# Opening modulation blocks in two halves, and another order of the steps in neighbourhood attention

## The reference

```python
shift, scale, gate = jnp.split(jax.nn.silu(cond) @ w_mod + b_mod, 3, axis=-1)   # cond: c or c_ctx
h = rms_norm(x, g_pre) * (1 + scale) + shift
(sg_u, sg_v, sg_gate, dq, dk, dv, d_gate, nq, nk, nv, n_gate, f_gate, merge) = split(h @ w_in)
y_sg   = spatial_gating(sg_u, sg_v, ...)            # A
y_diff = diff_attention(dq, dk, dv, lam)            # B
y_na   = neighbourhood_attention(nq, nk, nv, ...)   # C: 8 heads, 256 local keys per query tile + 128 cached
y_f    = fourier_mix(h)                             # D
mixed = sum over the branches of sigmoid(merge_i) * ((y_i * silu(gate_i)) @ p_i)
out = rms_norm(mixed @ w_o, g_post);   return x + gate * out
```

## Time and profile before

| | us |
|---|---|
| median of 3 runs | 2064.86 (2063.15 to 2065.28) |
| the profiled execution | 2058.49 |
| its span | 2056.4 |
| TensorE busy in it | 1963.3 |
| VectorE, ScalarE, GpSimd busy | 955.7, 647.1, 593.6 |

### The profile page before, as it was taken

How to read it: one execution, slowest core, us unless ns; L and a number is a source line. 1 busy time by engine, 2 the same in 40 slices (tenths; PEclk the granted TensorE clock), 3 DMA queues, 4 the chain that set the end, 5 groups by cost and what they waited for, 6 DMA issues and landing times.

```text
span 2056.4 us, 30590 instructions
## 1 busy us (share of the span) xinstructions
PE 1963.3 (95%) x12384; PEld 1782.0 (87%) x12384; DVE 955.7 (46%) x1480; ACT 647.1 (31%) x1101; POOL 593.6 (29%) x278
## 2 busy tenths in 40 slices
PE   6799989999999999999999999999999999999998
PEld 3698877889898999999878988888988899999996
DVE  5798666453444463421352143445344555443022
ACT  4323233323343321221352233333243332223121
POOL 2434311213222232233333332222322223313331
...
GB/s 294 151 158 145 127 101 31 42 52 93 61 64 52 62 102 62 52 72 81 125 101 94 88 72 62 42 42 42 83 72 62 57 58 99 66 51 72 72 111 74
DMA packets 50955, 172.13 MB, mean 84 GB/s; under 512 B 6656, under 2 KB 7296, under 8 KB 50816
## 3 DMA queue, kind: packets, MB, share of 16 engines
...
## 4 chain that ended last, share of the span: by engine, by line
PE 78%; DVE 14%; issue 4%; ACT 2%; DMA 1%; POOL 0%; SPq 0%; ACTq 0%; DVEq 0%; POOLq 0%
PE ps L1614 53%; PE ps L1502 4%; PE ps L1504 4%; PE ps L1503 4%; DVE mixed L1057 4%; PE ps L1688 3%; PE ps L1707 2%; PE ps L1726 1%; PE ps L1716 1%; DVE Pm L1328 1%; DVE nmax L1286 1%; ACT Pm L977 1%; DMA stage<-in_w_mod 1%; PE ps L1679 1%; PE ps L1689 1%
## 5 line engine op out<-in xcount | busy, mean ns | idle before, releaser
L728 POOL TENSOR_TENSOR wlo<-raw,whi 128x1024 fp32r<-128x1024 f32 x224 | 563.3, 2515 | 1319.7 <-ACT whi L786 1317.6
L1614 PE MATMUL ps<-bufB,whi 128*128 128x320 f32 x2816 | 541.8, 315 | 6.5 <-DVE vn L1183 4.0
L1614 PE MATMUL ps<-bufA,whi 128*128 128x320 f32 x2816 | 540.7, 314 | 4.9 <-DVE z L1448 1.4
L1614 PEld LDWEIGHTS ps<-bufB,whi 128*128 128x128 f32 x2816 | 443.5, 190 | 16.5 <-issue 11.5
L1614 PEld LDWEIGHTS ps<-bufA,whi 128*128 128x128 f32 x2816 | 442.3, 189 | 14.9 <-issue 10.1
L1614 PE MATMUL ps<-bufB,wlo 128*128 128x320 f32 x1408 | 323.4, 311 | 0.0
L1614 PE MATMUL ps<-bufA,wlo 128*128 128x320 f32 x1408 | 323.2, 311 | 0.0
L786 ACT ACTIVATE whi<-raw 128x1024 fp32r<-128x1024 f32 x224 | 237.6, 1061 | 210.5 <-PE ps L1614 125.0
L1614 PEld LDWEIGHTS ps<-bufB,wlo 128*128 128x128 f32 x1408 | 237.7, 190 | 0.0
L1614 PEld LDWEIGHTS ps<-bufA,wlo 128*128 128x128 f32 x1408 | 237.5, 189 | 0.0
L977 ACT ACTIVATE Pm<-ps,nmax 128x640 f32<-128x640 f32 (+2 forms) x160 | 100.0, 625 | 364.8 <-DVE nmax L1286 339.7
...
## 6 DMA issues: line engine op xcount, KB each, us to landing
raw<-in_wstream SPq DMA_DIRECT2D x224, 512.0 KB, 3.3
stage<-in_wstream SPq DMA_DIRECT2D x32, 512.0 KB, 4.5
stage<-in_w_mod SPq DMA_DIRECT2D x16, 512.0 KB, 15.2
out_y_sample<-X ACTq DMA_DIRECT2D x8, 512.0 KB, 2.7
...
X<-in_x_sample SPq DMA_DIRECT2D x4, 512.0 KB, 10.9
xres<-in_x_sample ACTq DMA_DIRECT2D x4, 512.0 KB, 5.8
xres<-out_y_sample ACTq DMA_DIRECT2D x4, 512.0 KB, 5.9
```

The source lines that it names most:

```text
L728: pool.tensor_tensor(wlo[:, s % SPLITS, :], raw[:, s % RAWS, :], whi[:, s % SPLITS, :].bitcast(F32), ALU.subtract).then_inc(sems["lo"], 1)
L1614: ins = pe.matmul(ps[:, 2 * b + n, 0:HALF], wt[:, cols], src[:, part, base + k, n * HALF:(n + 1) * HALF], start=k == 0 and wt is hi and pa ...
```

## The change

1. **Wide blocks.** The host packs each half as 256 columns of shift and 256 of scale: part 0 (four blocks, `wide 0` to `wide 3`) holds channel blocks 0 and 1, part 1 holds 2 and 3. `WIDE` is now 4 blocks per part. TensorE multiplies part 0 ahead of the steps, and part 1 in a new step `W2`; `Z2` turns part 1's columns; `DK 0` and `DK 1` finish two channel blocks each. Part 1's rows go to bank 5 and are copied by ScalarE in `W2`.
2. **SyncE's queue.** c_row, ctx_row, x, wide 0 to 3, raw 0, wm 0, wm 1, wide 4 to 7, raw 1, wm 2 to 7.
3. **The order of the opening.** `DK 0`, `HK 0`, `DD 0`, `HL 0`, `HK 1`, `DD 1`, `HL 1`, `TK 0`, `W2`, `TK 1`, `Z2`, `DK 1`, then k = 2 to 7, with two `DD` in k = 4 and 5 and no `TK` ahead of k = 4. Slot 1 is treated ahead of `HK 2` instead of `HK 1`.
4. **Neighbourhood attention.** A round is TP(u-2), S(u), filler, PV(u-2), NM(u), filler, perhaps YN.

```diff
-WIDE = KT
+WIDE = KT // 2
...
-        out += [s + (0,) for s in both("S", u)]
         if u:
             out += both("TP", u - 2)
-        out.append(None)
+        out += [s + (0,) for s in both("S", u)] + [None]
         if u:
             out += both("PV", u - 2)[:1]
-        out += late + [None, ("NM", u)]
+        out += [("NM", u), None] + late
...
-    add(0, ("DK",))
-    dots = iter([("DD", n) for n in range(len(FIRST))])
-    for k in range(KT):
-        add(0, ("HK", k), *[d for _, d in zip(range(1 + (k == 5)), dots)], ("HL", k))
-        if k >= 2:
+    add(0, ("DK", 0), ("HK", 0), ("DD", 0), ("HL", 0), ("HK", 1), ("DD", 1), ("HL", 1), ("TK", 0), ("W2",), ("TK", 1), ("Z2",), ("DK", 1))
+    dots = iter([("DD", n) for n in range(2, len(FIRST))])
+    for k in range(2, KT):
+        add(0, ("HK", k), *[d for _, d in zip(range(1 + (k > 3)), dots)], ("HL", k))
+        if k >= 4:
             add(0, ("TK", k - 2))
...
-        lead_in = [0, 1, 3, 5, 7]
+        lead_in = [0, 2, 3, 5, 7]
...
+            wide(0)
+            load_entry(0)
             for n in range(len(FIRST)):
-                if n in (0, 2):
-                    load_entry(n // 2)
-                sp.dma_start(staged(WIDE + n), A["w_mod"][:, WIDE + n, :]).then_inc(sems[f"wm{n}"], 16)
+                if n == 2:
+                    wide(1)
+                    load_entry(1)
+                sp.dma_start(staged(2 * WIDE + n), A["w_mod"][:, 2 * WIDE + n, :]).then_inc(sems[f"wm{n}"], 16)
...
+                    elif kind == "W2":
+                        act_e.wait_ge(sems["modrow"], 2)
+                        act_e.activation(modrows[1], ps[0:2, 5, :], ACT.Copy).then_inc(sems["modcopied"], 1)
+                        act_e.wait_ge(sems["modcopied"], 2)
...
+                        dve.wait_ge(sems["modready"], part + 1)
...
+            def wide(part, bank):
                 for k in range(KT):
-                    j = 4 * n + k // 2
+                    j = WIDE * part + k // 2
                     if k % 2 == 0:
                         pe.wait_ge(sems[f"wide{j}"], 16)
-                    ins = pe.matmul(ps[0:2, 7 - n, :], silc[:, k, :], staged(j)[:, k % 2 * 512:k % 2 * 512 + 512], start=k == 0, stop=k == KT - 1)
+                    ins = pe.matmul(ps[0:2, bank, :], silc[:, k, :], staged(j)[:, k % 2 * 512:k % 2 * 512 + 512], start=k == 0, stop=k == KT - 1)
                 ins.then_inc(sems["modrow"], 1)
...
+            wide(0, 7)
+            columns(0)
...
+                    elif kind == "W2":
+                        pe.wait_ge(sems["hfree"], count.step("hfree", ("HK", 0)))
+                        wide(1, 5)
+                    elif kind == "Z2":
+                        columns(1)
                     elif kind == "HK":
...
-                            pe.wait_ge(sems["modk"], count.step("modk", ("DK",)))
+                            pe.wait_ge(sems["modk"], count.step("modk", ("DK", 0)))
+                        if k == 2:
+                            pe.wait_ge(sems["modk"], count.step("modk", ("DK", 1)))
```

More of the change, by code:

```diff
@@ L497 @@
         "first", "crow", "pro", "early", "xload0", "xload1", "xload2", "xload3", "xload4", "setup", "tanhc", "silu", "rows",
-        "dload0", "dload1", "dload2", "dload3", "modk", "moddot", "modrow", "modcopied", "modready", "lamdot", "lamexp", "hfreed"] + [f"wide{n}" for n in range(WIDE)] + [f"wm{n}" for n in range(len(FIRST))]
+        "dload0", "dload1", "dload2", "dload3", "modk", "moddot", "modrow", "modcopied", "modready", "lamdot", "lamexp", "hfreed"] + [f"wide{n}" for n in range(2 * WIDE)] + [f"wm{n}" for n in range(len(FIRST))]
 UNFENCED = {"raw0", "raw1", "hi", "lo", "used"}
@@ L680, in _ @@
                 sp.dma_start(rows[:, c, :], A[n].partition_broadcast(P)).then_inc(sems["crow"], 16)
-            for j in range(WIDE // 2):
-                sp.dma_start(staged(j), A["w_mod"][:, j, :]).then_inc(sems[f"wide{j}"], 16)
             for j in range(TILES):
@@ L699, in load_entry, with wide @@
                 sp.dma_start(aside[n % ASIDE], A["wstream"][e]).then_inc(sems[f"dload{n % ASIDE}"], 16)
-            for j in range(WIDE // 2, WIDE):
-                sp.dma_start(staged(j), A["w_mod"][:, j, :]).then_inc(sems[f"wide{j}"], 16)
+            def wide(part):
+                for j in range(WIDE * part, WIDE * part + WIDE):
+                    sp.dma_start(staged(j), A["w_mod"][:, j, :]).then_inc(sems[f"wide{j}"], 16)
+            wide(0)
+            load_entry(0)
             for n in range(len(FIRST)):
-                if n in (0, 2):
-                    load_entry(n // 2)
-                sp.dma_start(staged(WIDE + n), A["w_mod"][:, WIDE + n, :]).then_inc(sems[f"wm{n}"], 16)
+                if n == 2:
+                    wide(1)
+                    load_entry(1)
+                sp.dma_start(staged(2 * WIDE + n), A["w_mod"][:, 2 * WIDE + n, :]).then_inc(sems[f"wm{n}"], 16)
             for dst, src in ((gpost[:], A["g_post"]), (colmask[:], A["colmask"]),
@@ L818, in _ @@
                     elif kind == "ZC":
[L819 to L822 removed]
+                        act_e.wait_ge(sems["modrow"], 1)
+                        act_e.activation(modrows[0], ps[0:2, 7, :], ACT.Copy).then_inc(sems["modcopied"], 1)
+                        act_e.wait_ge(sems["modcopied"], 1)
+                    elif kind == "W2":
+                        act_e.wait_ge(sems["modrow"], 2)
+                        act_e.activation(modrows[1], ps[0:2, 5, :], ACT.Copy).then_inc(sems["modcopied"], 1)
+                        act_e.wait_ge(sems["modcopied"], 2)
                     elif kind == "H":
@@ L842, in _ @@
                         h = hz[k % 2]
-                        act_e.wait_ge(sems["modk"], count.step("modk", ("DK",) if k < 4 else ("DD", 2 * (k - 4) + 1)))
+                        act_e.wait_ge(sems["modk"], count.step("modk", ("DK", k // 2) if k < 4 else ("DD", 2 * (k - 4) + 1)))
                         if k >= 2:
@@ L1114, in _ @@
                         dve.wait_ge(sems[f"wm{n}"], 16)
-                        for ins in dots(FIRST[n], staged(WIDE + n)):
+                        for ins in dots(FIRST[n], staged(2 * WIDE + n)):
                             ins.then_inc(sems["moddot"], 1)
@@ L1484, in _, with columns @@
             pe.wait_ge(sems["setup"], 2)
-            for n in range(2):
+            def wide(part, bank):
                 for k in range(KT):
-                    j = 4 * n + k // 2
+                    j = WIDE * part + k // 2
                     if k % 2 == 0:
                         pe.wait_ge(sems[f"wide{j}"], 16)
-                    ins = pe.matmul(ps[0:2, 7 - n, :], silc[:, k, :], staged(j)[:, k % 2 * 512:k % 2 * 512 + 512], start=k == 0, stop=k == KT - 1)
+                    ins = pe.matmul(ps[0:2, bank, :], silc[:, k, :], staged(j)[:, k % 2 * 512:k % 2 * 512 + 512], start=k == 0, stop=k == KT - 1)
                 ins.then_inc(sems["modrow"], 1)
-            for n, row in enumerate(modrows):
-                pe.wait_ge(sems["modcopied"], n + 1)
+            def columns(part):
+                pe.wait_ge(sems["modcopied"], part + 1)
                 for k in range(4):
-                    ins = pe.transpose(ps[:, 5, 8 * n + 2 * k:8 * n + 2 * k + 2], row[:, k * P:(k + 1) * P], ident[0:2, 0:2])
-            ins.then_inc(sems["modready"], 1)
+                    ins = pe.transpose(ps[:, 5, 2 * k:2 * k + 2], modrows[part][:, k * P:(k + 1) * P], ident[0:2, 0:2])
+                ins.then_inc(sems["modready"], 1)
+            wide(0, 7)
+            columns(0)
             if True:
@@ L1923 @@
     a["cond"] = np.stack([x["c"][0].reshape(KT, P).T, x["c_ctx"].reshape(KT, P).T], 2)
-    wide = [x["w_mod"][0, :, at:at + 512].reshape(KT, P, 512).transpose(1, 0, 2).reshape(P, 4, SLOT) for at in (0, D_MODEL)]
+    wide = [np.concatenate([x["w_mod"][0, :, at:at + 256], x["w_mod"][0, :, D_MODEL + at:D_MODEL + at + 256]], 1)
+            .reshape(KT, P, 512).transpose(1, 0, 2).reshape(P, 4, SLOT) for at in (0, 256)]
     a["w_mod"] = np.concatenate([*wide, modulation(np, x)[:, FIRST]], 1)
```

15 lines of the change are left out of this document (6 added, 9 removed).

## The result

The changed kernel takes 2049.11 us, the median of four runs (2048.54 to 2049.66), against 2064.01 for the kernel before on the same chip (2062.01 to 2065.28, four runs): a ratio of 0.9929, 95% interval 0.9914 to 0.9945, or 14.9 us less. The forecast was 2053.7 with a range of 2043 to 2064, 11.2 us less.

What follows compares the result with a forecast made beforehand. TensorE, busy 95% of the span, was taken as the bound, and VectorE's list of work in the opening. Opening +8.9 and neighbourhood attention -20.1 gave -11.2 us, from 2064.9 to 2053.7, range 2043 to 2064.

Steps and rivals of the forecast that it cites:

- Start of the opening: Opening: first half lands at 15.0, its batch takes 9.12 us, VectorE's list starts at 26.1, a gain of 3.0.
- The stall ahead of `DK 1`: Opening: VectorE idles over 12 us, 35.4 to 47.7, while TensorE runs `TK 0`, the second half's products and `TK 1`.
- The list behind `DK 1`: Opening: VectorE's work up to `HL 5` takes 28.7 us plus 0.4, ending at 77.4; the opening ends 8.9 later.
- The high bound: Opening: +12.7 us instead of +8.9, with products at the lower clock (2.1) and `TK 6` slow (1.7).
- ScalarE ahead of `HK 7`: Opening: ScalarE treats three slots first, 8.0 us; `HL 7` done by about 80, wanted at 86.6, so hidden.
- The waits for `NM`: Neighbourhood attention: all eleven waits of `TP` for `NM` go, -14.7 us; 2.0 us of new waits are added.
- The reason given for `PV`'s wait: Neighbourhood attention: 2.2 us of waits for ScalarE's copies go, since `TP` puts the copies ahead of the exponentials.
- The clock: Neighbourhood attention: three falls to half clock go with the longer waits for `NM`, 1.75 us each, 5.2 together.
- From one execution to the median: Whole kernel: the median lies 6.4 us above the profiled execution, so 2047.3 profiled goes with a median of 2053.7.
- The opening did not gain after all: Rival, chance 0.10: VectorE's wait for `DK 1` is short, the opening keeps its 3.0 us gain; -23 us, 2042.
- The new waits did not eat half: Rival, chance 0.20: `YN` and blocks hold `TP` and `PV`, clock stays low, opening costs 9 to 12; 2061 to 2068.
- `NM` too late in every round: Rival, chance 0.08, neighbourhood attention: 38 rounds of 0.6 us make 23 us of new waits; +10 us, 2075.

Runs made afterwards that it cites:

- early_second: The changed kernel with the second half's products and columns straight behind `HK 1`, ahead of `TK 0`; 2040.22 us, ratio 0.9905 to the kernel before.
- dots_in_gap: The changed kernel with `DD 2` to `DD 5` put ahead of `DK 1`; 2043.50 us, ratio 0.9926 to the kernel before.
- scales_ahead: The kernel before with only `NM` moved ahead of the second filler in neighbourhood attention; 2051.49 us, ratio 0.9958.
- after_again: The changed kernel measured again in a later set beside other kernels; 2048.0 us, ratio 0.9946 to the kernel before.
- na_only: The kernel before with only the new order of neighbourhood attention, old opening; 2040.64 us against 2060.07, ratio 0.9903.
- opening_only: The changed kernel with the old order of neighbourhood attention; 2066.88 us against 2060.07 for the kernel before, ratio 1.0033.
- na_again: The kernel of `na_only` measured in a second set; 2041.80 us against 2061.19 for the kernel before, ratio 0.9907.
- turns_first: The kernel before with only `TP` moved ahead of `S` in neighbourhood attention, `NM` still last; 2082.59 us, ratio 1.0108.

## Why the prediction was right, step by step

**Start of the opening: right, 1.0 too small.** The first half landed at 14.73 (15.0 forecast), but its batch took 8.45 and not the 9.12 of the old first one. Both batches begin with slow products, about 1.05 us where the later ones take 0.59: five in the old batch and four in the new one, one of them 0.79. (The view gives a granted clock of 1.00 there, so only the lengths show it.) The dots start at 25.02, 4.0 ahead of before; 3.0 were forecast. `early_second`, whose batch is the same, has seven slow products and took 9.71, so this term moves by over a us from one execution to another, and the 1.0 gained here is luck.

**The stall ahead of `DK 1`: right.** 12.88 us, "over 12" in the prediction; `DK 1` done at 47.79 against 48.3. `early_second`, which ends it by another place for the products, wins 7.8 us, and `dots_in_gap`, which fills it with dots, 4.5: it is the order of the steps that costs.

**The list behind `DK 1`: right.** 28.8 us from 47.79 to the end of `HL 5` at 76.6, against 28.7 + 0.4; four blocks met it, as forecast. 0.5 less at `DK 1` and 0.3 less in the list make +8.1 of the forecast +8.9. The low bound, blocks falling on idle time, did not come. The high bound, slow clock, did come in part: the granted clock from 20 to 100, in windows of 20 us, is 0.83, 0.91, 0.72, 0.94 now and was 0.75, 1.00, 0.83, 1.00. It cost little, as VectorE was the bound up to 76.6.

**ScalarE ahead of `HK 7`: right that it was hidden, by little.** `HL 7` ended at 80.4 (80 forecast). `dots_in_gap` shows what it costs when the list is shorter: 9.30 us of VectorE.

**The waits for `NM`: right.** -14.7 - 2.2 + 2.0 was forecast, and the rows give just that: 2.0 in 4 places are left. The cause of these was half right. The four are the same two rounds in each layer (0.64 and 0.38 us), with a block on `NM`, as said; no wait at `YN`'s new place is in the list. One of the four:

```profile
524.40 2.40 POOL L730 TENSOR_TENSOR wlo<-raw,whi 128x1024 fp32r<-128x1024 f32 x1 [7.72 <-ACT whi L788]
...
524.65 2.82 DVE L1335 TENSOR_SCALAR Pm<-Pm,rsum 128x384 f32<-128x384 f32 x2
...
527.53 0.88 PE L1726 MATMUL ps<-ident,Pm 128*128 128x128 f32 x6 [0.64 <-DVE Pm L1335]
```

Two L1335 take 2.82 where an undisturbed pair takes 0.88, and end 0.67 behind GpSimd's L730 (526.80). Such a block of 1.9 us is nearly all covered by the slack of 2.0. The Trainium skill (SBUF — State Buffer, "Who interferes with whom") says that a `tensor_scalar` can use the port pair that VectorE shares with GpSimd, and that whoever issues second is then blocked fully; this row agrees: L730 started 0.25 us ahead of the two L1335.

**The reason given for `PV`'s wait: too narrow.** The 2.2 us of the copies were taken as a small item that `TP` first happens to remove. `scales_ahead` shows that they grow to 11.4 when `NM` alone moves up. The sum was right only because the change has both halves; that is luck.

**The clock: nearly right, and a small cost was left out.** In the profiled executions attention gave 10.1 + 8.2 = 18.3; the waits make up 14.7 + 2.2 - 2.0 = 14.9 of it, so 3.4 are left where 5.2 were counted for three falls of the clock. TensorE is busy all through the windows of 1 us at 0.50, so they are not idle time that costs nothing:

```profile
556.00:557.00 1.00, 1.00 (x7) 1.00 (x6) 0.93 (x3) 0.22 (x1) 0.00 (x0) 0.50 0.00 0
...
638.00:639.00 1.00, 1.00 (x5) 1.00 (x5) 0.93 (x2) 0.67 (x2) 0.00 (x0) 0.50 0.71 283
```

What a fall costs can be read in the kernel before: the same round stands in both layers behind the same wait, with a fall in layer 0 and none in layer 1.

```profile
636.90 0.98 PE L1707 MATMUL ps<-ident,Pm 128*128 128x128 f32 x6 [2.13 <-DVE Pm L1328]
...
649.47 0.87 PE L1707 MATMUL ps<-ident,Pm 128*128 128x128 f32 x6
...
1632.34 0.88 PE L1707 MATMUL ps<-ident,Pm 128*128 128x128 f32 x6 [2.14 <-DVE Pm L1328]
...
1643.36 0.87 PE L1707 MATMUL ps<-ident,Pm 128*128 128x128 f32 x6
```

From one `TP` to the next it takes 12.57 with the fall and 11.02 without, so a fall costs 1.55, not 1.75, and three cost 4.7. The rest is a price of the new order that the prediction did not have. A round without waits, from `PV` to `PV`, before and now:

```profile
1568.19 0.66 PE L1726 MATMUL ps<-AT,V 128*64 128x128 f32 x8
...
1579.66 0.66 PE L1726 MATMUL ps<-AT,V 128*64 128x128 f32 x8
```

```profile
1562.12 0.66 PE L1745 MATMUL ps<-AT,V 128*64 128x128 f32 x8
...
1573.63 0.66 PE L1745 MATMUL ps<-AT,V 128*64 128x128 f32 x8
```

That is 11.47 and 11.51 us; 0.04 in each of 38 rounds is about 1.5 us (an estimate from these rows). 14.9 + 4.7 - 1.5 = 18.1, near the 18.3. Why a round takes 0.04 more is not shown.

**From one execution to the median: the step that failed.** The prediction worked out -11.2 between profiled executions and carried the 6.4 us between that execution and the median over to the changed kernel unchanged. The changed kernel's median lies only 0.6 above its profiled execution, and 0.4 in `after_again`. So the step put 5.8 too much on; 1.2 the other way come from the profiled execution (2048.54 against 2047.3), which leaves the 4.6 between 2053.7 and 2049.11. Nor do the 6.4 hold for the kernel before: in the four later sets, 36 runs, its median stood 1.2 to 2.7 above 2058.49. That the forecast of -11.2 missed the set of the result by 3.7 and met `after_again` (-11.7) within 0.5 hangs on how the runs of before fell, and is luck.

What moves them is told in part by the granted clock that each run of the later sets lists (those of before in the set of the result are not on record):

| kernel (runs at 0.982 and 0.983 left out) | at 0.984 or 0.985 | at 0.979 to 0.981 |
|---|---|---|
| before, 13 runs in the set of `na_only` | 2056.07, 2057.55, 2058.28, 2060.38, 2060.76 | 2059.95, 2060.82, 2065.02, 2065.68 |
| opening_only, 8 runs | 2064.75 to 2065.92 | 2069.42, 2070.05 |
| scales_ahead, 6 runs (the last at 0.980) | 2049.56 to 2049.66 | 2056.32 |
| changed kernel, all 9 runs (one at 0.986) | 2046.39 to 2049.66 | none |

Kernels with long waits in attention have a lower mean clock in some of their executions, and in sets of six runs and more they spread by 5 to 10 us. From 0.984 to 0.979 is 0.005 of 2056 us, about 10 us of clock (an estimate), and the fastest and slowest run of before are 9.6 apart. The changed kernel never fell so low in nine runs. It is not a clean rule. `na_again`, without the waits, had one run at 0.982 (2043.96, against 2038.45 at 0.986), and `turns_first`, with the longest waits, spread by only 2.2 at 0.978 to 0.981. The clock also varies where no step was changed: from 1050 to 1110, with the same waits of 3.9 and 3.4 us, the granted clock was 0.94 in `na_only` and 0.89 in `na_again`. So the link with the waits is a correlation, and its cause is not shown.

**The rivals.** The opening did not gain after all (`opening_only`). The new waits did not eat half. In `scales_ahead` they did, with `YN` ahead of the maxima as the rival named, but through copies that stand behind the exponentials, which it did not name. `NM` too late in every round did not come with the change; it is what `turns_first` shows, +22.3, for it moves `TP` up against an `NM` that stays.
